# An encoder trunk's first RMSNorm taken from the feature-major input on GpSimd, and the token rows loaded later

## The reference

```python
def rmsnorm(x, g):
    xf = x.astype(jnp.float32)
    y = xf * lax.rsqrt(jnp.mean(xf * xf, axis=-1, keepdims=True) + NORM_EPS)
    return (y * g.astype(jnp.float32)).astype(x.dtype)

h = rmsnorm(x, norm_mix_g[0])
x = x + even_mixer(h, w_in_even[0], w_fnet[0], w_out_even[0], rel_bias_table)
```

## Time and profile before

| what | us |
|---|---|
| median of 3 executions | 2164.16 |
| lowest and highest | 2164.1, 2164.45 |
| the profiled execution's own time | 2164.72 |
| its span in the profile | 2162.9 |
| TensorE busy | 2153.2 |
| VectorE busy | 1389.1 |
| ScalarE busy | 1021.8 |
| GpSimd busy | 15.9 |

### The profile page before, as it was taken

The page is one execution under the profiler, slowest core; times in us unless marked ns, Lnnn a source line. Parts: engine busy times, 40 slices in busy tenths (PEclk is TensorE's granted clock), DMA queues, the critical chain, the costliest instruction groups (busy, mean ns, idle before and its releaser), DMA issues.

```text
span 2162.9 us, 30895 instructions
## 1 busy us (share of the span) xinstructions
PE 2153.2 (100%) x11160; PEld 1837.7 (85%) x11160; DVE 1389.1 (64%) x1945; ACT 1021.8 (47%) x1442; POOL 15.9 (1%) x31
## 2 busy tenths in 40 slices
PE   9999999999999999999999999999999999999998
PEld 7888888888888888888888888888888888888887
DVE  6777756755764665675577777657646656755754
ACT  6444445544543443454445445454434434444543
POOL 1000000000000000000000000000000000000000
PEclk9999999999999999999999999999999999999999
DMA  9544456555555555555544444545555555555553
GB/s 355 205 164 168 158 184 223 186 195 186 192 194 195 186 188 192 191 194 182 187 176 175 175 159 173 195 175 194 194 193 180 192 195 194 183 195 185 193 194 117
DMA packets 63347, 408.92 MB, mean 189 GB/s; under 512 B 6724, under 2 KB 12356, under 8 KB 15262
## 3 DMA queue, kind: packets, MB, share of 16 engines
q1 hardware_dynamic: 60046, 402.46, 52.1%
q10 hardware_dynamic: 2656, 3.44, 0.5%
q0 software_dynamic: 560, 1.84, 0.2%
HBM read 405.58 MB, written 2.14 MB: 189 GB/s over the span
## 4 chain that ended last, share of the span: by engine, by line
PE 98%; DMA 1%; issue 0%; ACT 0%; SPq 0%; DVE 0%; POOL 0%; POOLq 0%; DVEq 0%; ACTq 0%
PE acc L1073 32%; PE acc L1077 16%; PE ps_scores L1106 7%; PE ps_scores L1107 7%; PE ps_scores L1105 7%; PE ps_v L1105 4%; PE ps_v L1106 4%; PE ps_v L1107 4%; PE acc L1106 2%; PE acc L1107 2%; PE acc L1105 2%; PE ps_aux L1105 2%; PE ps_aux L1106 2%; PE ps_aux L1107 2%; PE ps_o L1164 1%; PE ps_scores L1164 1%
## 5 line engine op out<-in xcount | busy, mean ns | idle before, releaser
L661 DVE TENSOR_TENSOR w_lo<-raw,w_hi 128x1024 fp32r<-128x1024 f32 x744 | 908.4, 1223 | 520.7 <-ACT w_hi L363 518.0
L363 ACT ACTIVATE w_hi<-raw 128x1024 fp32r<-128x1024 f32 x744 | 787.1, 1058 | 633.4 <-PE ps_scores L1107 253.9
L1073 PE MATMUL acc<-gx,w_hi 128*128 128x512 f32 x3008 | 947.0, 396 | 0.0
L1077 PEld LDWEIGHTS acc<-gx,w_lo 128*128 128x128 f32 x3008 | 565.0, 188 | 133.2
L1077 PE MATMUL acc<-gx,w_lo 128*128 128x256 f32 x3008 | 591.3, 278 | 0.0
L1073 PEld LDWEIGHTS acc<-gx,w_hi 128*128 128x128 f32 x3008 | 460.2, 189 | 2.2 <-DVE w_lo L661 0.2
L1105 PE MATMUL ps_scores<-w_hi,mid 128*128 128x512 f32 x640 | 249.5, 390 | 0.0
L1107 PE MATMUL ps_scores<-w_hi,mid 128*128 128x512 f32 x640 | 249.0, 389 | 0.0
L1106 PE MATMUL ps_scores<-w_lo,mid 128*128 128x512 f32 x640 | 249.0, 389 | 0.0
L370 ACT ACTIVATE copied<-acc 128x256 f32<-128x256 f32 x188 | 72.0, 383 | 316.3 <-PE acc L1077 316.3
L694 DVE TENSOR_TENSOR head<-acc,copied 128x256 f32<-128x256 f32 x188 | 79.8, 424 | 176.2 <-ACT copied L370 174.7
(11 more groups left out here) (198 smaller groups left out, 1629.0 us busy)
## 6 DMA issues: line engine op xcount, KB each, us to landing
raw<-weights_dram SPq DMA_DIRECT2D x372, 1024.0 KB, 4.8
raw<-opening_dram SPq DMA_DIRECT2D x6, 512.0 KB, 8.9
x<-x_tok_dram SPq DMA_DIRECT2D x2, 1024.0 KB, 15.1
bias<-bias_line SPq DMA_DIRECT2D x2, 1024.0 KB, 9.6
bias<-bias_line ACTq DMA_DIRECT2D x2, 1024.0 KB, 8.7
bias<-x_fm_dram SPq DMA_DIRECT2D x6, 256.0 KB, 8.9
bias<-bias_line SPq DMA_DIRECT2D x2, 512.0 KB, 5.9
bias<-final_gain_dram POOLq DMA_DIRECT2D x1, 1024.0 KB, 7.0
```

Of the source, the lines that this page charges most:

```text
L363: act.activation(w_hi[:, n % RING, :], raw[:, u % RAW_SLOTS, part * HALF:(part + 1) * HALF], ACT.Copy).then_inc(hi_ready, 1)
L661: dve.tensor_tensor(w_lo[:, n % RING, :], raw[:, u % RAW_SLOTS, part * HALF:(part + 1) * HALF], w_hi[:, n % RING, :].bitcast(F32), ALU.sub ...
L1073: pe.matmul(acc[w % 2][:], w_hi[:, n % RING, j * P:(j + 1) * P], gx[:, kt, :], start=kt == 0, stop=False)
L1077: ins = pe.matmul(acc[w % 2][:, SEQ:], w_lo[:, n % RING, i * P:(i + 1) * P], gx[:, kts[i], 0:SEQ], start=False, stop=kts[i] == KT - 1)
```

## The change

The first norm is taken from `x_first` instead of `x`. GpSimd squares the k-tiles four at a time, as their chunks land, into `x_squares` (room of `x`), adds the four blocks and folds them to one of 256 columns; TensorE multiplies that by a column of ones (`token_sums`, hooked into the second half of the first narrow unit), and VectorE scales the sums. ScalarE's `first_squares` go. SP issues the token rows behind the rest of the bias, once `sums_ready` says that the squares are read. The bias table, its constant row and the one-hot matrix become one array, loaded by ScalarE's queue; the bias product moves from behind k-tile 2 to behind k-tile 1, the copy of its line from behind k-tile 5 to behind k-tile 3, and ScalarE's queue issues the line's store. The identity, the lambdas and the gains are issued by GpSimd behind its second block. The lambda sum moves from the second narrow unit to the first values quarter. The values of the opening are split ahead of half 12 and no longer ahead of half 14. Chunk (4, 6) becomes (4, 5) and (5, 6), and WARM goes from 12 to 10.

```diff
--- before.py
+++ after.py
@@ -39,9 +39,9 @@
 OPEN = 4
 N0 = 2 * OPEN
 OPEN_RING = RING * HALF // WIDE
-CHUNKS = ((0, 1), (1, 2), (2, 3), (3, 4), (4, 6), (6, 8), (8, 10), (10, 12), (12, 14), (14, 16))
+CHUNKS = ((0, 1), (1, 2), (2, 3), (3, 4), (4, 5), (5, 6), (6, 8), (8, 10), (10, 12), (12, 14), (14, 16))
 CHUNK_OF = {lo: c for c, (lo, hi) in enumerate(CHUNKS)}
-WARM = 12
+WARM = 10
 
 V_HEADS0, V_HEADS1 = 4, 2
 LEAN1 = C_HEADS - V_HEADS1
@@ -109,7 +109,7 @@
 Y_ACT = ((0, 0, D // 2), (1, 0, 6 * P))
 
 
-def trunk(nc, first_x, x_fm, x_tok, opening, weights, final_gain, subln, lambdas, table, w_fnet, onehot, a_head_row,
+def trunk(nc, first_x, x_fm, x_tok, opening, weights, final_gain, subln, lambdas, positions, w_fnet,
           channel_dft, position_dft, identity, out):
     ctx = ExitStack()
     with ctx:
@@ -139,7 +139,8 @@
         hi_open = w_hi[:].rearrange("p r (a c) -> p (r a) c", c=WIDE)
         lo_open = w_lo[:].rearrange("p r (a c) -> p (r a) c", c=WIDE)
         line = bias[0:HEADS, 0, :, :].rearrange("h t k -> h (t k)")
-        one_hot = bias[0:BUCKETS + 1, 1, :, :].rearrange("b t k -> b (t k)")
+        table_rows = bias[0:BUCKETS + 1, 1:3, :, :].rearrange("b h t k -> b (h t k)")
+        one_hot, tab = table_rows[:, 0:LINE], table_rows[:, LINE:LINE + HEADS]
         head = sb("head", [P, 4 * KT + SEQ])
         gain = head[:, 0:4 * KT].rearrange("p (n k) -> p n k", n=4)
         sub_gain = sb("sub_gain", [P, 2])
@@ -149,7 +150,6 @@
         lam_exp = sb("lam_exp", [P, 2])
         lam_diff = sb("lam_diff", [P, 1])
         neg_lam = sb("neg_lam", [P, 1])
-        tab = sb("tab", [BUCKETS + 1, HEADS])
         pos_dft = sb("pos_dft", [P, QT, 2, SEQ])
         ch_map = sb("ch_map", [P, GROUPS, 2, P])
         mixed = sb("mixed", [P, QT, 2 * P])
@@ -163,6 +163,7 @@
         square = sb("square", [P, SEQ])
         proj_full = relu
         squares_out = mixed[:].rearrange("p t c -> p (t c)")
+        x_squares = x[:].rearrange("p t (b c) -> p (t b) c", b=2)
         rstd = sb("rstd", [P, SEQ])
         token_parts = sb("token_parts", [P, QT, COL_GROUPS + 1])
         mean_sq = sb("mean_sq", [P, QT])
@@ -225,6 +226,7 @@
         gx_hi, gx_ready = sem("gx_hi"), sem("gx_ready")
         first_rows_done, last_rows_done = sem("first_rows_done"), sem("last_rows_done")
         x_done, turned = sem("x_done"), sem("turned")
+        x_folded, sums_ready = sem("x_folded"), sem("sums_ready")
         sq_done = sem("sq_done")
         mean_ready, inv_ready = sem("mean_ready"), sem("inv_ready")
         bcast_ready, rstd_ready = sem("bcast_ready"), sem("rstd_ready")
@@ -290,18 +292,17 @@
                     sp.dma_start(raw_open[:, lo:hi, :], opening[:, lo:hi, :]).then_inc(open_landed[c], 16)
                 if c:
                     sp.dma_start(x_first[:, lo:hi, :], x_fm[:, lo:hi, :]).then_inc(x_landed[c], 16)
-            load(4)
-            load(5)
-            for t in range(QT):
-                sp.dma_start(x[:, t, :], x_tok[:, t, :]).then_inc(tokens_landed[t], 16)
-            sp.wait_ge(line_copied, 1)
-            sp.dma_start(bias_line, line).then_inc(line_stored, 16)
-            load(6)
+            for u in range(OPEN, 7):
+                load(u)
             sp.wait_ge(line_stored, 16)
             load_bias(sp, bias_first, 0, 0, BIAS_FIRST)
             for u in range(7, OPEN + 2 * RAW_SLOTS):
                 load(u)
+            sp.wait_ge(sq_done, SQUARES)
             load_bias(sp, bias_rest, BIAS_FIRST, BIAS_FIRST, A_HEADS)
+            sp.wait_ge(sums_ready, 1)
+            for t in range(QT):
+                sp.dma_start(x[:, t, :], x_tok[:, t, :]).then_inc(tokens_landed[t], 16)
             with sp.Fori(2, UNITS // RAW_SLOTS - 1) as i:
                 for s in range(RAW_SLOTS):
                     load(RAW_SLOTS + s, RAW_SLOTS * i)
@@ -317,12 +318,33 @@
             pool.memset(ones[:], 1.0)
             pool.memset(token_parts[:, :, COL_GROUPS:], EPS)
             pool.memset(minus_half[:], -0.5).then_inc(ones_ready, 1)
-            pool.dma_start(tab[0:BUCKETS, :], table).then_inc(tab_landed, 16)
-            pool.dma_start(tab[BUCKETS:BUCKETS + 1, :], a_head_row).then_inc(tab_landed, 16)
-            pool.dma_start(one_hot, onehot).then_inc(tab_landed, 16)
-            pool.dma_start(ident[:], identity).then_inc(small_landed, 16)
-            pool.dma_start(lam_in[:], lambdas).then_inc(small_landed, 16)
-            pool.dma_start(sub_gain_in[:], subln).then_inc(small_landed, 16)
+
+            def add_squares(b, cols, count):
+
+                pool.wait_ge(x_folded, count)
+                pool.tensor_tensor(x_squares[:, 0, 0:cols], x_squares[:, 0, 0:cols], b, ALU.add).then_inc(x_folded, 1)
+
+            for b in range(KT // 4):
+                for k in range(max(4 * b, 1), 4 * b + 4):
+                    if k in CHUNK_OF:
+                        pool.wait_ge(x_landed[CHUNK_OF[k]], 16)
+                if b == 0:
+                    pool.wait_ge(x_landed[0], 16)
+                    pool.tensor_tensor(x_squares[:, 0, 0:SEQ], summed, summed, ALU.mult).then_inc(sq_done, 1)
+                k = max(4 * b, 1)
+                rows = x_first[:, k:4 * b + 4, :].rearrange("p k c -> p (k c)")
+                pool.tensor_tensor(x_squares[:, b, (k - 4 * b) * SEQ:], rows, rows, ALU.mult
+                                   ).then_inc(sq_done, QT if b else 1)
+                pool.wait_ge(sq_done, QT * (b + 1))
+                if b:
+                    add_squares(x_squares[:, b, :], 4 * SEQ, b - 1)
+                if b == 1:
+                    pool.wait_ge(open_lo, KT // 2)
+                    pool.dma_start(ident[:], identity).then_inc(small_landed, 16)
+                    pool.dma_start(lam_in[:], lambdas).then_inc(small_landed, 16)
+                    pool.dma_start(sub_gain_in[:], subln).then_inc(small_landed, 16)
+            add_squares(x_squares[:, 0, 2 * SEQ:4 * SEQ], 2 * SEQ, 3)
+            add_squares(x_squares[:, 0, SEQ:2 * SEQ], SEQ, 4)
             pool.wait_ge(open_lo, KT)
             pool.dma_start(wf[:], w_fnet.rearrange("g c e -> c g e")).then_inc(dft_landed, 16)
             pool.dma_start(ch_dft, channel_dft).then_inc(dft_landed, 16)
@@ -456,6 +478,7 @@
 
             act.dma_start(head[:], first_x).then_inc(x_landed[0], 16)
             act.dma_start(raw_open[:, 1:2, :], opening[:, 1:2, :]).then_inc(open_landed[1], 16)
+            act.dma_start(table_rows[:, 0:LINE + HEADS], positions).then_inc(tab_landed, 16)
             act.wait_ge(ones_ready, 1)
             act.activation(first_act[:], ones[:, 0:1], ACT.Copy)
 
@@ -477,22 +500,14 @@
                 else:
                     hi_gx(N_MIX0, k, x_first[:, k, :])
                     open_hi_part(k)
-                if k == 5:
+                if k == 3:
                     act.wait_ge(line_ready, 1)
                     act.activation(line, scores_flat[0][0:HEADS, :], ACT.Copy).then_inc(line_copied, 1)
-
-            def first_squares(t):
-
-                act.wait_ge(tokens_landed[t], 16)
-                for g in range(COL_GROUPS):
-                    square_tokens(COL_GROUPS * t + g, t, g)
-
-            split_hi(8)
-            split_hi(9)
-            first_squares(0)
-            split_hi(10)
-            first_squares(1)
-            split_hi(11)
+                    act.wait_ge(line_copied, 1)
+                    act.dma_start(bias_line, line).then_inc(line_stored, 16)
+
+            for n in range(N0, N0 + RING):
+                split_hi(n)
 
             def copy_maps():
 
@@ -528,8 +543,8 @@
             for h in range(A_HEADS):
                 u, w, g = head0_unit(h), head0_narrow(h), h - MIX_HEAD0
                 if h == 0:
-                    narrow(u, w)
-                    narrow(u + 1, w + 1, before=[values_hi(0, 0, 0)])
+                    narrow(u, w, before=[values_hi(0, 0, 0)])
+                    narrow(u + 1, w + 1)
                 else:
                     mixing = g > 0
                     narrow(u, w, first=[copy_mixed(g - 1)] if mixing else [],
@@ -746,6 +761,8 @@
                             dve.wait_ge(first_rows_done, G + 1 + oG)
                         else:
                             dve.wait_ge(w_used, 2 * u_last + 2 - N0 + 2 * o)
+                        if isinstance(oG, int) and G + oG < COL_GROUPS:
+                            dve.wait_ge(tokens_landed[t], 16)
                         dve.tensor_tensor(x[:, t, columns(g)], x[:, t, columns(g)], banks[g][t], ALU.add
                                           ).then_inc(x_done, 1)
                 return step
@@ -814,10 +831,12 @@
             dve.wait_ge(small_landed, 16 * 3)
             dve.tensor_tensor(lam_prod[:], lam_in[:, 0:4:2], lam_in[:, 1:4:2], ALU.mult).then_inc(lam_steps, 1)
             dve.tensor_scalar(sub_gain[:], sub_gain_in[:], 1.0 - LAMBDA_INIT, None, ALU.mult).then_inc(lam_steps, 1)
+
             split_lo(8)
             split_lo(9)
             split_lo(10)
```

(33 more changed lines are left out.)

## The result

The changed kernel takes 2174.22 us (median of 6, 2173.55 to 2175.57) against 2164.18 us of the kernel before in the same session (6 runs, 2163.66 to 2164.84): ratio 1.0046, 95% interval 1.0036 to 1.0056. It is 10 us slower. The profiled execution has a span of 2172.7 us, 9.8 more than before. What was forecast was 2162.5; what came is the first rival, priced at 2173.6.

The account below looks back on a forecast made before the run. TensorE, busy for all but ten of 2162.9 us, was taken as the bound. Terms -0.55 - 1.23 - 0.12 - 0.19 + 0.4 = -1.7 us gave 2162.5 us from the median 2164.16; range 2161.3 to 2170.0.

Parts of the forecast that it names:

- the first rival: In the opening, VectorE and GpSimd exclude each other for whole instructions when reading SBUF: 2173.6 us, chance 0.18.
- The start: Two fewer warm-up products let the first real products run earlier: 0.55 us won, bounds 0 and 0.86.
- The clock's rise: TensorE's step from 1.2 GHz to full speed was taken to stay at about 6.6 us despite the shorter warm-up.
- The bias product, the copy and the issues on ScalarE, the small loads: Moved work and loads in the opening: the bias product keeps its 1.1 us, and the moves cost 0.
- The price of GpSimd's work: Squares and additions for the first norm: 2.1 ns a column, 2.15 us for 1024 columns, ten instructions 16.7 us.
- All 0, covered by VectorE's and ScalarE's lead: Opening edits cost nothing, as VectorE needs 1.00 us a k-tile and TensorE 1.37.
- the condition (1.37 us a k-tile): Exclusion decides once VectorE needs over 1.37 us a k-tile in the opening; each 0.1 above costs 1.2 us.
- The chain of the norm: Behind the opening, waits for root (1.23), unit 10 (0.12) and first values (0.19) go if GpSimd's sums are in time.
- The token sums: Two added fp32 products with one column on TensorE, in the first narrow unit: 0.4 us, bounds 0.28 and 0.75.
- rival 2: GpSimd is slowed while VectorE keeps its lead; TensorE stands 5.4 us at the token sums: 2167.9 us, chance 0.13.
- The token rows behind the bias: On SP's queue, token rows move from 17.01 to near 50, needed only in the output projection: cost 0.

Follow-up runs that it names:

- the best version: Changed kernel with ScalarE making the squares, VectorE the additions and half 10 split behind them, GpSimd only the power: 2162.93 us, ratio 0.9994 to the kernel before.
- the run with these edits alone: Changed kernel with the norm taken from the token rows as before, loaded behind unit 5's weights, and all other edits kept: 2166.19 us, ratio 1.0008.
- the phases measured alone: Separate kernel without the trunk: phases of eight VectorE instructions beside two of GpSimd; two-SBUF sum loses 3.4 us beside a two-input product, nothing beside a memset.

## Why the prediction was wrong

**The start:** right in size. The first product comes at 5.42, k-tile 6 of the opening at 15.36 against 15.90 before: 0.54 us, forecast 0.55. The size is shown to a few tenths only: where nothing held VectorE, the opening ended 0.3 to 0.8 us earlier than before (29.16 to 28.68). With WARM back at 12 the best version is 0.5 us longer in span and 0.3 in the median. The clock's rise did not stay where it was: the full pace is there from 6.36 in the changed kernel and from 6.73 before, so part of the agreement is luck.

**The bias product, the copy and the issues on ScalarE, the small loads:** no wait of TensorE in the changed kernel ends on them. The bias product stands at 8.76 and k-tile 2 follows at 9.72, so its 1.0 us is only moved one k-tile ahead. Since the run with these edits alone lost 1.9 us for a cause that stayed open, "cost nothing" is shown for the waits and, by the 2162.93 us of the last version, which keeps them, for the sum; it is not shown for each alone.

**The price of GpSimd's work:** forecast 2.15 us for 1024 columns. Where VectorE holds nothing, a product of a tile with itself takes 1.9 (3.75 for two) and an addition 2.35, 2.1 in the mean. Right.

**"All 0, covered by VectorE's and ScalarE's lead": this step failed.** It took VectorE's 1.00 us a k-tile as given while a second engine began to read SBUF beside it. VectorE's work was longer by 12.7 us (36.78 against 24.12), not by 0. The lead of 0.37 us a k-tile is real and was used up in the second block: TensorE's first wait, 2.43 us, is for k-tile 6, whose w_lo ended at 18.35. The forecast named the condition (1.37 us a k-tile) and the mechanism, and gave it 0.18. The Trainium skill (SBUF — State Buffer, Who interferes with whom) states the exclusion for exactly these two kinds of instruction; the phases measured alone agree with it in each case, the length of the hold (3.4 us to 3.75 us of GpSimd's work) as well as its absence beside a memset. It should have been the forecast.

**The rival's own sum,** 2173.6 against 2174.22, had the mechanism right; that the total is so close is partly luck, since its terms erred both ways. VectorE's instructions became 14.1 us longer, for 14.5 and more, but 1.4 us of that fell into waits that VectorE had anyway, and its end moved by 12.7. TensorE was to end four products behind VectorE, 0.9 us; it ended 3.6 behind (40.42 against 36.78), because it had two and a half k-tiles still to do after running at its lower clock. The rival did not price the clock. An estimate from the rows: twelve products from 31.30 to 36.58 took 5.28 us where twelve at 0.228 take 2.74, so the lower clock made 2.5 of the 10.9 us by which the opening ended later, and the hold by itself the rest.

**The chain of the norm:** right in form. The waits for the root, half 10 and the values are gone, 1.5 us less between the end of the opening and the values quarter with the token sums already paid, and 0.2 of it the lambda sum that moved. The token sums cost 0.36 us and 0.09 on the products behind, 0.45 for 0.4. GpSimd's sums were ready at 33.2 and TensorE asked at 44.6, so rival 2 never came up: what slows VectorE slows the one who asks.

**The token rows behind the bias:** cost nothing that a wait shows.

## What to carry to other kernels

An idle engine is not free: before GpSimd is given arithmetic, look at what VectorE does at that time, and if it reads two operands from SBUF (or scales or copies within SBUF), add the full length of GpSimd's instructions to VectorE's; beside a two-operand instruction those that only write are free, beside a scale or copy they are not. Where work must go off a bound path, ScalarE or an idle stretch of VectorE itself took it here without a loss. Many short pieces that start as early as they can cost less than few long ones, 2169.1 against 2174.2 us here: VectorE's idle time at the start is used, and TensorE's waits stay so short that its clock stays at 1.00. How much of it is the size alone was not tried. And a wait of TensorE costs more than its length when the clock falls behind it: 2.5 us here.

## What the runs showed of the hardware

- A memset on GpSimd leaves VectorE's two-SBUF sum alone (4.91 us with and without), but two of 1024 columns hold a scale or copy from SBUF to SBUF (4.42 us instead of 2.78).
- The exclusion works both ways. GpSimd's power of two columns, 0.74 us, takes 1.56 in the changed kernel at 45.45, beside a w_lo that starts at 45.21 and takes 1.22; the change itself put that w_lo there. The root is ready at 47.01 and spread at 47.82, so no wait came of it.
- The profile's granted clock reads 1.00 over the warm-up while its weight loads take 331 ns against 188 later, yet it reads 0.83 and 0.66 over the windows of the changed kernel that hold its slow stretches. At the start the durations have to be read, not the clock.
